# A two-block network on one core: the w_hi products of both merged units ahead of the w_lo products of both

## The reference, cut to what matters

```
def conv_ffn(h, w_up, w_conv, b_conv, w_down):          # w_up 1024 x 5632, w_down 2816 x 1024
    u = h @ w_up
    u = conv(u, w_conv, width 3, one filter per channel) + b_conv
    val, gate = jnp.split(u, 2, axis=-1)
    return (jax.nn.silu(gate) * val) @ w_down

def shortconv_mixer(h, w_in, conv_w, w_out):            # w_in 1024 x 6144, w_out 1536 x 1024
    bg, cg, xv, gate = the four quarters of h @ w_in
    y = bg * causal_depthwise_conv(cg * xv, conv_w)
    return (y * jax.nn.silu(gate)) @ w_out
```

## Time and profile before

| | |
|---|---|
| median of 3 runs | 865.6 us (864.5 to 865.66) |
| profiled execution, its span | 866.1 us |
| TensorE matmul busy | 854.8 us, 99% |
| VectorE busy | 677.1 us, 78% |
| ScalarE busy | 542.4 us, 63% |
| merged units' products with w_hi (L1796) | 944 |
| merged units' products with w_lo (L1800) | 944 |
| weights loaded | 134 units of 1 MB and 12 halves |

### The profile page before, as it was taken

The page is one execution under the profiler, slowest core; times in us unless marked ns, Lnnn a source line. Parts: engine busy times, 40 slices in busy tenths (PEclk is TensorE's granted clock), DMA queues, the critical chain, the costliest instruction groups (busy, mean ns, idle before and its releaser), DMA issues.

```text
span 866.1 us, 13361 instructions
## 1 busy us (share of the span) xinstructions
PE 854.8 (99%) x4881; PEld 749.8 (87%) x4881; DVE 677.1 (78%) x970; ACT 542.4 (63%) x746; POOL 38.8 (4%) x57
## 2 busy tenths in 40 slices
PE   7999999999999999999999999999999999999997
PEld 7988889888888888889888888989999898888886
DVE  6899767887886798878788787787987877776764
ACT  5745656656656576576675655567988765555533
POOL 1000100000000032000000000000011100000000
PEclk9999999999999999999999999999999999999999
DMA  7544543676555445134666655435364046545511
GB/s 265 210 151 190 195 145 104 237 230 248 194 194 194 146 146 194 62 134 146 243 213 218 229 193 212 173 112 229 123 252 162 0 148 243 209 183 214 214 53 50
DMA packets 22909, 152.82 MB, mean 176 GB/s; under 512 B 2608, under 2 KB 2736, under 8 KB 5712
## 3 DMA queue, kind: packets, MB, share of 16 engines
q1 hardware_dynamic: 22176, 149.45, 47.7%
q0 software_dynamic: 544, 2.49, 0.9%
q10 hardware_dynamic: 144, 0.26, 0.1%
HBM read 151.14 MB, written 1.05 MB: 176 GB/s over the span
## 4 chain that ended last, share of the span: by engine, by line
PE 94%; DMA 2%; DVE 2%; ACT 1%; issue 1%; SPq 0%; ACTq 0%; DVEq 0%
PE acc L1864 30%; PE ring L1796 24%; PE ring L1800 12%; PE ring L1849 10%; PE ring L1811 3%; PE acc L2085 3%; PE ring L1935 1%; DMA raw<-in_stream_dram 1%; PE ring L1830 1%; PE ring L2067 1%; PE ring L2243 1%; PE acc L1758 1%; PE ring L2125 1%; DMA wr<-in_wr_dram 1%; DVE w_lo L1005 1%
## 5 line engine op out<-in xcount | busy, mean ns | idle before, releaser
L1005 DVE TENSOR_TENSOR w_lo<-raw,w_hi 128x2048 fp32r<-128x2048 f32 (+1 forms) x145 | 317.9, 2197 | 5.4 <-ACT w_hi L511 5.4
L511 ACT ACTIVATE w_hi<-raw 128x2048 fp32r<-128x2048 f32 (+1 forms) x146 | 266.9, 1840 | 56.3 <-DMA raw<-in_stream_dram 53.0
L1796 PE MATMUL ring<-hh,w_hi 128*128 128x512 f32 x944 | 235.9, 392 | 0.2 <-DVE usum L1123 0.2
L1796 PEld LDWEIGHTS ring<-hh,w_hi 128*128 128x128 f32 x944 | 171.3, 189 | 32.3 <-DVE usum L1123 0.6
L1800 PEld LDWEIGHTS ring<-hh,w_lo 128*128 128x128 f32 x944 | 128.8, 190 | 9.2
L1800 PE MATMUL ring<-hh,w_lo 128*128 128x256 f32 x944 | 131.6, 282 | 0.0
L1864 PE MATMUL acc<-w_hi,a_hi 128*128 128x512 f32 x264 | 103.9, 394 | 0.3 <-DVE a_lo L1689 0.3
L1864 PE MATMUL acc<-w_lo,a_hi 128*128 128x512 f32 x264 | 103.1, 390 | 0.0
L1864 PE MATMUL acc<-w_hi,a_lo 128*128 128x512 f32 x264 | 102.8, 389 | 0.0
L1123 DVE TENSOR_TENSOR usum<-ring,usum 128x512 f32<-128x512 f32 x65 | 44.7, 688 | 56.8 <-ACT usum L516 56.6
L1849 PE MATMUL ring<-hh,w_hi 128*128 128x256 f32 x480 | 87.8, 285 | 0.0
(11 more groups left out here) (249 smaller groups left out, 968.5 us busy)
## 6 DMA issues: line engine op xcount, KB each, us to landing
raw<-in_stream_dram SPq DMA_DIRECT2D x134, 1024.0 KB, 4.8
raw<-in_stream_dram SPq DMA_DIRECT2D x12, 512.0 KB, 4.0
gatew<-in_gatew_dram POOLq DMA_DIRECT2D x4, 384.0 KB, 4.2
x<-in_x_dram SPq DMA_DIRECT2D x2, 512.0 KB, 3.7
out_dram<-xn SPq DMA_DIRECT2D x3, 256.0 KB, 2.6
row<-in_row_dram POOLq DMA_DIRECT2D x1, 640.0 KB, 5.3
gup_raw<-in_gup_dram SPq DMA_DIRECT2D x3, 128.0 KB, 11.5
par<-in_par_dram SPq DMA_DIRECT2D x1, 274.0 KB, 4.7
```

The source lines that it names most:

```text
L511: nc.scalar.activation(w_hi[:, u % RING, 0:n], raw[:, u % RAW, 0:n], ACT.Copy).then_inc(hi_split, 1)
L1005: nc.vector.tensor_tensor(w_lo[:, u % RING, 0:n], raw[:, u % RAW, 0:n], w_hi[:, u % RING, 0:n].bitcast(f32), ALU.subtract).then_inc(lo_spl ...
L1796: nc.tensor.matmul(ring[:, 2 * k + f, :], w_hi[:, u % RING, lo:lo + P], hh[:, kc, :, :], start=kc == 0, stop=False, skip_group_check=True)
```

## The change

In `merged` the loop over blocks f held both kinds of products. It is taken apart into `merged_high` (the waits, and the products with `w_hi` of both blocks) and `merged_low` (those with `w_lo`, and the raising of `used`). `up` and `sc_up` now issue the high products of the first unit, those of the second, the low products of the first, those of the second. In the last up of a stage the first unit's high and low products come in turn and then the wide unit. The waits are the same ones, with the high products.

```diff
-            def merged(u, k, i=0, done=None):
+            def merged_high(u, k, i=0, done=None):
 
                 ready(u, i)
                 if done is not None:
...
                         lo = kc * 256 + f * P
                         nc.tensor.matmul(ring[:, 2 * k + f, :], w_hi[:, u % RING, lo:lo + P], hh[:, kc, :, :],
                                          start=kc == 0, stop=False, skip_group_check=True)
+
+            def merged_low(u, k):
+
+                for f in range(2):
                     for kc in range(KC):
...
                 def up(e, i=0):
-                    for k in range(2):
-                        if (e, k) == (FFN_ITERS - 1, 1):
-                            wide(ffn_unit(B, e, k), 2, free=(summed, M + 2 * e))
-                        else:
-                            merged(ffn_unit(B, e, k), k, i, done=M + 2 * e + k - 1 + 4 * i)
+                    end = e == FFN_ITERS - 1
+                    for k in range(1 if end else 2):
+                        merged_high(ffn_unit(B, e, k), k, i, done=M + 2 * e + k - 1 + 4 * i)
+                    for k in range(1 if end else 2):
+                        merged_low(ffn_unit(B, e, k), k)
+                    if end:
+                        wide(ffn_unit(B, e, 1), 2, free=(summed, M + 2 * e))
```

More of the change, by code:

```diff
@@ L2267, in sc_up @@
             def sc_up(e, i=0):
[L2268 to L2272, removed]
+                end = e == SC_ITERS - 1
+                for k in range(1 if end else 2):
+                    merged_high(sc_unit(e, k), k, i, done=SUM_SC + 2 * e + k - 1 + 4 * i)
+                for k in range(1 if end else 2):
+                    merged_low(sc_unit(e, k), k)
+                if end:
+                    wide(sc_unit(e, 1), 2, free=(summed, SUM_SC + 2 * e))
             def sc_down(e, u, i=0, tiles=range(T), halves=(0, 1)):
```

## The result

| | before | after |
|---|---|---|
| median of 5 runs, us | 865.57 (864.24 to 865.66) | 873.97 (871.59 to 875.3) |
| ratio, 95% interval | | 1.0094 (1.0082 to 1.0106) |
| span of the profiled execution, us | 866.1 | 872.8 |

The kernel became 8.4 us slower where 5.8 was forecast; the median lies 0.5 us above the range. The direction and the three places of loss were as forecast. One term was far too small, the restart behind a wait: behind two of the three new waits the granted clock falls.

What follows compares the result with a forecast made beforehand. The prediction took the kernel as a queue of matmuls, TensorE busy 99% of the span. Pace -1.3, tails +5.2 and short convolution +1.9 summed to +5.8 us, so 871.4 from a median of 865.6; range 866.0 to 873.5.

Steps and rivals of the forecast that it cites:

- the three places of loss: Forecast new TensorE waits: the tail of each of the two feed-forward layers, and the start of the short convolution.
- Pace: Up calls: fewer w_hi runs behind w_lo gain 0.06 us per call; 22 of 28 calls count, -1.3 us.
- Tails: End of both feed-forward layers: late first cross delays a_lo, stalling TensorE 2.6 us each with restart; +5.2 us.
- Short convolution: Its start, step 2: TensorE reaches the second unit earlier and waits 2.3 us for its sum; +1.9 us.
- Restart after a wait: Feed-forward tails: the first run of products behind a TensorE wait is slower, 0.1 us.
- Hidden steps: Caught-up feed-forward steps: the later first cross stays covered, with 4 us to spare and no TensorE wait.
- Base: Whole kernel: the runs' median, 865.6, taken as 0.5 us under the profiled span of 866.1.
- B: Rival: tails given back, a later stage absorbs the delay; +0.6, 866.2 us; chance 0.10.
- B': Rival: tails partly given back, idle time absorbs 1 to 2 us in each; 867.4 to 869.4 us; chance 0.10.
- C: Rival: waits hidden anyway, only pace left in all 28 calls; faster, 863.3 us; chance 0.06.
- D: Rival: late splits delay loads in the short convolution, 0.4 us in each of 8 steps; 874.6 us; chance 0.12.

Runs made afterwards that it cites:

- e7: Kernel before, with a merged unit's runs of 8 + 8 products cut into 4 + 4 + 4 + 4: 867.04 us against 865.09, ratio 1.0021.
- e11: Kernel before, with w_hi of both blocks, then w_lo of both, inside each merged unit: 864.42 us against 865.48, ratio 0.9986.
- e5: Kernel before, with the new order only in up(9) of both feed-forward layers: 872.96 us against 865.09, ratio 1.0089.
- e9: The kernel before, unedited, run again for a second trace (also called the control): 865.55 us against 865.48, ratio 1.0; traced span 863.8 us.
- e8: Kernel before, with the new order only in up(2) of the short convolution: 868.28 us against 865.09, ratio 1.0029.
- e6: Changed kernel, old order in the short convolution's up(2), ten unread products before each feed-forward tail's waiting product: 870.15 us against the kernel before's 865.09, ratio 1.0057.
- e3: Changed kernel, with the old order in up(9) of both feed-forward layers: 870.45 us against the kernel before's 865.8, ratio 1.0044.
- e4: Changed kernel, old order in up(9) of both feed-forward layers and up(2) of the short convolution: 867.3 us against the kernel before's 865.8, ratio 1.0015.
- e10: Changed kernel, old order in up(8), up(9) of both feed-forward layers and the short convolution's up(2): 864.92 us against the kernel before's 865.48, ratio 0.9994.

## Why the prediction was wrong in size and right in mechanism

- *Pace, -1.3:* right. The step is 0.06 shorter, as forecast (the sum 32 x 0.227 + 32 x 0.12 is 11.10 and would have given 0.05), and e7 and e11 show the sign from both sides. Their rival, that a product's time goes by its own columns, which would have made it 0, falls for this kernel.
- *Tails, +5.2:* the chain was right to 0.1 us (a_lo's end at +21.9 against a forecast of 22.0; stalls of 2.44 and 2.45 from start to start for 2.5). From up(10)'s start to the next layer's up(1) the second tail costs 2.5 us (158.38 for 155.85), for 2.6 with the restart. The first costs 3.95 (121.84 for 117.89), 1.4 of it by the clock. e5 shows that these two calls carry it.
- *Short convolution, +1.9:* right but for the clock (a stall of 2.27 from start to start, 724.77 to 727.27 less 0.227, for 2.3). Up(2) became 3.45 us longer (721.27 to 736.46, in e9 715.24 to 726.98), and without the clock's 1.6 that is 1.85; e8 shows that one call carries it.
- *Restart after a wait, 0.1 us:* this is the term that failed. It came from the run at 723.54 in the earlier trace rows, which follows an idle time of 0.23 us. A wait of 2.3 us is another case: behind two of the three waits of the trace the granted clock fell, 1.5 and 1.6 us more. With them 5.8 + 3.1 = 8.9, against 9.0 between the spans of the control and of the changed kernel. Between the median spans it is 7.6, so the middle execution loses 1.8 us beyond the forecast, about one fall of the clock. Behind the third wait 0.1 was right. e6 shows that filling the wait keeps the clock up. Of the rivals none held this. Why the clock falls behind one wait and not behind an equal one is not shown.
- *Hidden steps:* no wait inside steps 3 to 9, right as to TensorE. But "hidden" was only read within a step. A late cross of step 8 alone makes that of step 9 late, as e3, e4 and e10 show; in the changed kernel this made no difference, since there the unit itself was later.
- *Base, 0.5 us between span and median:* read as one effect, but two nearly cancelled. The first trace is of an execution some 2 us longer, and about 1.8 us lie around a span. As the forecast was a difference put on the median, the error did not pass into it.
- *The rivals:* neither B nor B', the tails given back in whole or in part, happened: at the next layer's up(1) each tail's loss is there in full. C, only the pace, did not either, nor D, more waits in the short convolution. The time came out near D's 874.6 all the same, through the clock.

## What to carry to other kernels

When TensorE has no slack, an order of its products is to be judged by when each result is finished for the engines behind it: follow a late result through their queues to the end of the stage, and over several steps if the queue's period is near TensorE's. Price a new wait of TensorE of 2 us with the clock's fall behind it (1.5 us here, in some executions and not in others; behind waits of 0.9 us it did not fall), and if it can't be avoided, try work in it. Taking single calls back can move a wait to the next one. The gain of equal widths in a row was had here without any lateness, by regrouping only within a unit.

## What was not expected of the hardware

A single wait of about 2 us between long runs of products cost TensorE its clock in nine of ten cases in the traces: it was 0.50 for 3.4 us, which cost about 1.5 us. Behind the tenth, as long as the others, it stayed. The changed kernel's five runs reach over 3.7 us, those of the kernel before over 1.4. And a run of 512-column products is slower behind 256-column ones: 1.83 us for eight instead of 1.81, paid once per change. In the down unit the operands change at every product, at no such price.
